# Queries of both mixers projected turned, partitions exchanged by DMA, keys rotated from memory

## The reference

```
h = rms_norm(x); proj = h @ w_in       # 1024 x 3072
a_u, a_v, b_q, b_k, b_v, b_g, c_q, c_k, c_v = split(proj)
y_a = gmlp_mixer(a_u, a_v)             # 4 heads of 64, 128x128 mixing per chunk
y_b = retention_mixer(b_q, b_k, b_v, b_g)   # 6 heads of 64, rope on all 64
y_c = swa_sink_mixer(c_q, c_k, c_v)    # 6 query heads, 2 kv heads, window 128, rope on 16 of 64
x += rms_norm([y_a|y_b|y_c] @ w_out)
x += rms_norm((silu(gate) * up) @ w_ffn_out)
x += sigmoid(x @ w_gate) * rms_norm(p @ w_ple)
```

## Time and profile before

| | |
|---|---|
| median of 3 runs | 1225.25 us |
| profiled execution | 1225.42 us, span 1223.7 us |
| TensorE busy | 1217.0 us, 99% |
| VectorE busy | 841.5 us, 69% |
| ScalarE busy | 616.0 us, 50% |
| GpSimd busy | 136.6 us, 11% |
| HBM read | 118.90 MB, 99 GB/s over the span |

### The profile page before, as it was taken

The page is one execution under the profiler, slowest core; times in us unless marked ns, Lnnn a source line. Parts: engine busy times, 40 slices in busy tenths (PEclk is TensorE's granted clock), DMA queues, the critical chain, the costliest instruction groups (busy, mean ns, idle before and its releaser), DMA issues.

```text
span 1223.7 us, 20397 instructions
## 1 busy us (share of the span) xinstructions
PE 1217.0 (99%) x7873; PEld 1109.8 (91%) x7873; DVE 841.5 (69%) x1365; ACT 616.0 (50%) x1204; POOL 136.6 (11%) x208
## 2 busy tenths in 40 slices
PE   9999999999999999999999999999999999999998
PEld 8988888999999988888899889889999999888887
DVE  5685646888888853267976756468988887433788
ACT  7454435555555532237664544364655555422474
POOL 2003621100000000003030037020000000000120
PEclk9999999999999999999999999999999999999999
DMA  7322232233333354320242222231333333444001
GB/s 247 111 65 91 70 103 69 70 104 104 104 105 106 109 183 154 124 67 18 86 119 73 91 75 90 74 103 53 104 105 106 108 101 119 163 147 172 18 18 70
DMA packets 124464, 122.31 MB, mean 100 GB/s; under 512 B 5200, under 2 KB 108752, under 8 KB 124368
## 3 DMA queue, kind: packets, MB, share of 16 engines
q1 hardware_dynamic: 123680, 120.48, 31.4%
q10 hardware_dynamic: 688, 0.53, 0.2%
HBM read 118.90 MB, written 2.10 MB: 99 GB/s over the span
## 4 chain that ended last, share of the span: by engine, by line
PE 98%; DVE 1%; ACT 0%; POOL 0%; issue 0%; DVEq 0%; ACTq 0%
PE bank L1004 31%; PE bank L1006 30%; PE bank L1005 30%; PE bank L1214 2%; PE bank L1273 1%; PE bank L1294 1%; PE bank L1333 1%; PE bank L1317 1%; PE bank L1309 0%; PE bank L1281 0%; PE bank L1329 0%; PE bank L1338 0%; PE bank L1224 0%; PE bank L1359 0%; PE bank L1255 0%; DVE ple_n L2196 0%
## 5 line engine op out<-in xcount | busy, mean ns | idle before, releaser
L1004 PE MATMUL bank<-w_hi,h_hi 128*128 128x384 f32 (+2 forms) x564 | 200.4, 355 | 0.8 <-DVE w_lo L1893 0.7
L1005 PE MATMUL bank<-w_lo,h_hi 128*128 128x384 f32 (+2 forms) x564 | 194.6, 345 | 0.0
L1891 DVE TENSOR_TENSOR w_lo<-raw,w_hi 128x1024 fp32r<-128x1024 f32 x70 | 83.6, 1233 | 133.7 <-ACT w_hi L1411 133.5
L1004 PE MATMUL bank<-h_hi,w_hi 128*128 128x256 f32 x568 | 161.0, 284 | 0.1
L1006 PE MATMUL bank<-h_hi,w_lo 128*128 128x256 f32 x568 | 160.7, 283 | 0.0
L1005 PE MATMUL bank<-h_lo,w_hi 128*128 128x256 f32 x568 | 160.7, 283 | 0.0
L1006 PE MATMUL bank<-w_hi,h_lo 128*128 128x384 f32 (+2 forms) x468 | 157.5, 336 | 0.0
L1411 ACT ACTIVATE w_hi<-raw 128x1024 fp32r<-128x1024 f32 x70 | 70.6, 1053 | 160.7 <-PE bank L1006 160.6
L1006 PE MATMUL bank<-w_hi,mid_lo 128*128 128x512 f32 x352 | 137.0, 389 | 0.0
L1004 PE MATMUL bank<-T_hi,w_hi 128*128 128x256 f32 x448 | 126.8, 283 | 0.0
L1005 PE MATMUL bank<-T_lo,w_hi 128*128 128x256 f32 x448 | 126.8, 283 | 0.0
(11 more groups left out here) (294 smaller groups left out, 2909.3 us busy)
## 6 DMA issues: line engine op xcount, KB each, us to landing
raw<-in_w_ffn_in SPq DMA_DIRECT2D x88, 512.0 KB, 3.9
raw<-in_w_ffn_out SPq DMA_DIRECT2D x44, 512.0 KB, 4.2
raw<-in_w_in SPq DMA_DIRECT2D x40, 384.0 KB, 3.8
raw<-in_w_out SPq DMA_DIRECT2D x16, 512.0 KB, 3.8
gw<-in_w_gate SPq DMA_DIRECT2D x16, 512.0 KB, 3.4
raw<-in_w_in SPq DMA_DIRECT2D x10, 512.0 KB, 4.6
raw<-in_w_ple SPq DMA_DIRECT2D x4, 512.0 KB, 5.9
x<-in_x_in SPq DMA_DIRECT2D x3, 512.0 KB, 6.9
```

Source lines behind the costliest of these rows:

```text
L1004: pe.matmul(out_ap, a_hi, b_hi, start=start, stop=False, skip_group_check=True)
L1005: pe.matmul(out_ap, a_hi, b_lo, start=False, stop=False, skip_group_check=True)
L1891: last = dve.tensor_tensor(lo, raw[q % RAWS][:, cols], hi, ALU.subtract)
```

## The change

The queries of both mixers are projected turned. On the host the columns of `w_in` are put in another order: a, bk, bv, bg, cq (its heads in pairs), bq, ckv. The 768 query columns make three groups qa, qb, qc of 256, each one strip over all 1024 rows, in place of cq and bq with two strips each; a layer has 12 `w_in` strips where it had 13. In `mm_turned` 128 weight columns are stationary and the tokens, 512 columns of `h_hi` and `h_lo`, move: a block's result has head dimensions on partitions. There are six blocks, in banks 0 to 3 in turn. The order of groups is ckv, qa, qb, qc, bk, bv, a, bg.

ScalarE copies each block to `q_raw`; four transfers by SP write it to `q_turn` with the halves of each head exchanged (8 or 32 partitions each, the rest of `q_turn` is zero from GpSimd); VectorE multiplies q_raw by a table of cosines (ones where nothing rotates), q_turn by a table of signed sines, and adds. The tables, 4 x 256 KB, are new inputs, loaded each layer. Results stand in cT and in the new qT. The norm's scale of the window queries moves from the copy to the exponential's scale and the maximum's factor (`s_q`, `s_qn`, two GpSimd operations for each tile).

`swa_T` transposes only the four tiles of ck, at once, in slot 8; `ret_T` only the keys. bk is copied out by ScalarE and rotated from memory by VectorE (`k_rope`) in slots 24, 26, 30 and 32. The retention's steps stand two slots earlier, gMLP's four and more, and the end of the mixer is rearranged. In the second layer the first block is taken in two parts, columns 0 to 383 (`q_most`) before the last tile of ckv, the rest after it; the conversion of the first query strip is in two halves. The other edits are places in memory and semaphores.

```diff
+    for i in range(2 * len(TURNED)):
+        put((6, 8, 10, 12, 16, 17)[i], "q_rope", i)
+    put(8, "swa_T")
     for c in range(TILES):
-        put(10 + c, "swa_T", c)
...
-            put(u + (1 if c < 3 else 2), "swa_yhi", c - 1)
+            put(u + 1, "swa_yhi", c - 1)
...
-            put(u + (1 if c < 2 else 2), "swa_ylo", c - 1)
+            put(u + (1 if c != 2 else 2), "swa_ylo", c - 1)
         put(u + (2, 1, 2, 2)[c], "swa_norm", c)
+        put(u + (5, 4, 4, 5)[c], "swa_mask", c)
         put(u + 5, "swa_PT", c)
-        put(u + (5, 5, 3, 5)[c], "swa_mask", c)
...
-        u = (33, 37, 41, 45)[c]
+        u = (31, 35, 39, 43)[c]
...
-        put(41 + c, "gmlp_v", c)
-        put(42 + c, "gmlp_n", c)
+        put(37 + c if c < 3 else 41, "gmlp_v", c)
+        put(38 + c if c < 3 else 42, "gmlp_n", c)
+        put((24, 26, 30, 32)[c], "k_rope", c)
     for c in range(TILES):
-        put(48 + c, "ret_norm", c)
-        put(50 + c, "ret_yT", c)
+        put(44 + c if c < TILES - 1 else 48, "ret_norm", c)
+        if c < TILES - 1:
+            put(46 + c, "ret_yT", c)
...
         add("gmlp_mix")
         mm(o[0], 1)
+        add("ret_yT", TILES - 1)
         mm(o[1], 1)
...
             mm(ins[0], 2, nxt)
+            add("q_most", lay=nxt)
+            mm(ins[0], 3, nxt)
             mm(ins[1], 0, nxt)
             mm(ins[1], 1, nxt)
-            mm(ins[0], 3, nxt)
...
+                if 3 <= s < 5:
+                    i = s - 3
+                    if layer:
+                        sp.wait_ge(g_mm, g_count(layer - 1, 4))
+                        sp.wait_ge(x_new, x_count(layer - 1, "gate", 3))
+                    sp.dma_start(cos_q[i][:], turns[2 * i]).then_inc(turns_loaded[i], 16)
+                    sp.dma_start(sin_q[i][:], turns[2 * i + 1]).then_inc(turns_loaded[i], 16)
...
+                if 6 <= s < 6 + len(TURNED):
+                    for i in (2 * s - 12, 2 * s - 11):
+                        b = i % 2
+                        half = HD // 8 if i < 3 else HD // 2
+                        sp.wait_ge(q_evac, 6 * layer + i + 1)
+                        for r in (0, HD):
+                            for d in (r, r + half):
+                                src = 2 * r + half - d
+                                sp.dma_start(q_turn[b][d:d + half, :],
+                                             q_raw[b][src:src + half, :]).then_inc(q_turned[b], 16)
...
+                    if name == "bk":
+                        pe.wait_ge(q_evac, 6 * layer + (5, 6, 3, 4)[m])
...
+            def mm_turned(layer, i, half, cols):
+
+                g = layer * NS + SIDX[("in", TURNED[i // 2], 0)]
+                if half == 0 and i < 4:
+                    pe.wait_ge(*evac(layer, "ckv", i))
+                elif half == 0:
+                    pe.wait_ge(q_evac, 6 * layer + i - 3)
+                pe.wait_ge(h_lo_ready, h_count(layer, "mix", (cols.stop - 1) // P, half))
+                pe.wait_ge(lo_ready, 2 * g + 1 + half)
+                hi, lo = (w[slot_of(g)][:, :].rearrange("p (k c) -> p k c", k=KD) for w in (w_hi, w_lo))
+                c = slice(i % 2 * P, i % 2 * P + P)
+                for k in range(4 * half, 4 * half + 4):
+                    last = mm3(banks[i % 4][:, cols], hi[:, k, c], lo[:, k, c], h_hi[:, k, cols], h_lo[:, k, cols],
+                               k == 0, k == KD - 1)
+                return last
...
+                    if name in TURNED and m % 2:
+                        i = 2 * TURNED.index(name) + m // 2
+                        n = 6 * layer + i + 1
+                        b = i % 2
+                        act.wait_ge(mm_done, mm_count(layer, strip, m))
+                        if n > 2:
+                            act.wait_ge(q_roped, n - 2)
+                        if i < 2:
+                            act.wait_ge(q_zeroed, 2 * layer + i + 1)
+                        act.activation(q_raw[b][:], banks[i % 4][:, :], ACT.Copy).then_inc(q_evac, 1)
...
+                elif kind == "q_rope":
+                    i = e[1]
+                    n = 6 * layer + i + 1
+                    b, which = i % 2, i // 3
+                    dst = (cT, qT)[which][:, i % 3, :]
+                    dve.wait_ge(q_evac, n)
+                    if i % 3 == 0:
+                        dve.wait_ge(turns_loaded[which], 32 * (layer + 1))
+                    dve.tensor_tensor(dst, q_raw[b][:], cos_q[which][:], ALU.mult)
+                    dve.wait_ge(q_turned[b], 64 * (3 * layer + i // 2 + 1))
+                    step(dve.tensor_tensor(q_turn[b][:], q_turn[b][:], sin_q[which][:], ALU.mult))
+                    done(dve.tensor_tensor(dst, dst, q_turn[b][:], ALU.add), q_roped)
```

More of the change, by code:

```diff
@@ L402, in build_trunk @@
                 post_mix, pre_ffn, w_ffn_in, w_ffn_out, post_ffn, w_gate, w_ple, ple_norm,
-                table, later, out):
+                table, later, turns, out):
     KB = 1024
@@ L533, in build_trunk @@
     gmu = small(4)
-    gvar = small(4)
+    gvar = [small(4) for _ in range(2)]
     gvt = small(4)
@@ L577, in build_trunk @@
     evac_act = sem("evac_act")
-    evac_dve = sem("evac_dve")
     ck_roped = sem("ck_roped")
-    cq_roped = sem("cq_roped")
+    turns_loaded = [sem(f"turns_loaded{i}") for i in range(2)]
+    q_evac = sem("q_evac")
+    q_turned = [sem(f"q_turned{i}") for i in range(2)]
+    q_roped = sem("q_roped")
+    q_scaled = sem("q_scaled")
+    q_zeroed = sem("q_zeroed")
     b_roped = sem("b_roped")
@@ L1161, in block_of @@
                     pe.wait_ge(lo_ready, 2 * (g + 1))
-                if kind == "in":
+                if kind == "in" and strip[1] in TURNED:
+                    block = 2 * TURNED.index(strip[1]) + m // 2
+                    last = mm_turned(layer, block, m % 2, slice(S - P if layer and block == 0 else 0, S))
+                elif kind == "in":
                     last = mm_in(layer, g, strip, m)
@@ L1246, in _ @@
                     gate_product(layer, e[1], e[2:] or (0, 1))
+                elif kind == "q_most":
+                    for half in range(2):
+                        mm_turned(layer, 0, half, slice(0, S - P))
                 elif kind == "swa_T":
[L1249 to L1258, removed]
+                    pe.wait_ge(ck_roped, (layer + 1) * TILES)
+                    for c in range(TILES):
+                        last = pe.transpose(banks[6][:, c * P:(c + 1) * P], ck[:, c, :], T_("ident"))
+                    last.then_inc(swa_T, 1)
                 elif kind in ("swa_cur", "swa_prev"):
@@ L1306, in _ @@
                         pe.wait_ge(y_lo_ready, y_count(layer, ("swa_o", 2)))
[L1307 to L1310, removed]
+                    for j in range(3):
+                        last = pe.transpose(banks[4][:, j * P:(j + 1) * P], bk[:, c, j * P:(j + 1) * P], T_("ident"))
                     last.then_inc(ret_T, 1)
@@ L2385 @@
     depth = w_in.shape[0]
-    table, later = small_tables()
+    table, later, turns = small_tables()
     values = {
@@ L2396 @@
         "w_gate": w_ple_gate, "w_ple": w_ple_proj, "ple_norm": ple_norm,
[L2397 removed]
+        "table": table, "later": later, "turns": turns,
     }
```

163 lines of the change are left out of this document (89 added, 74 removed).

## The result

The changed kernel takes 1231.44 us, the median of 9 runs (1227.22 to 1233.47), the kernel before 1225.25 (9 runs, 1225.08 to 1225.55). The ratio is 1.0043, 95% interval 1.0033 to 1.0052: slower. I had forecast 1220.9, range 1219.2 to 1224.0, and given "slower" 0.08. The profiled execution took 1231.63 us with a span of 1229.5.

What follows compares the result with a forecast made beforehand. TensorE, busy 1217.0 of 1223.7 us, was taken to bound the kernel. Its savings of 3.13 and 1.84 us by layer (-4.97), plus 0.6 for holes, gave -4.4: a median of 1220.9 us, range 1219.2 to 1224.0.

Steps and rivals of the forecast that it cites:

- The sum without the hole ahead of ret_yT: TensorE's savings on query products and transposes less the split block's cost: -3.13 us first layer, -1.84 second, -4.97 together.
- my +0.6: End of the mixer: TensorE waits 0.3 us a layer for y_lo of tile 0 before tile 1's ret_yT, +0.6 in all.
- The 14 ns fixed part: TensorE: each product pays 0.014 us whatever its columns; 48 fewer query products a layer save 0.67 us.
- rival (d): Query products on TensorE: fixed part not saved with 512-column moving queries, -0.24 in place of -1.34, 1222.0 us; chance 0.05.
- (c): Second layer's split block: short products cost as much as whole ones, +4.2 instead of +1.29, 1223.8 us; chance 0.06.
- (e): No holes anywhere, and the split block's short products at 0.0725 us each: -5.8 us, 1219.5 us; chance 0.14.
- rival (a): q_turn transfers land late, so TensorE waits at slot 17; at 9.3 us landing time +5.0, 1230.2 us; chance 0.11.
- (b): Small holes: slot 17 or the last transposes expose about 1 us a layer more, 1222.9 us; chance 0.14.
- L: Landing time of a query block's transfers inside SBUF, taken as 3 us; no hole until 4.6.
- The cover at slot 17: bk's product with tile 1 needs block 5's bank, copied out behind tile 0's exponentials; 1.1 us to spare.
- The step that failed: VectorE and ScalarE lose 8 query rotations, gain 18 operations; keys rotated in slots 24 to 32 for use from 31.
- the split's 1.29 us: Second layer's first block in two parts costs TensorE +1.29 us, with 24 short products at 0.107 each.

Runs made afterwards that it cites:

- the keys in the gaps: The changed kernel with the four key rotations moved to the ends of slots 24, 24, 29 and 29, where VectorE stood idle: 1221.0 us, ratio 0.9963.
- The run: The changed kernel with key rotations in VectorE's idle time, and the second layer's first query block taken whole, no filler ahead: 1219.77 us, ratio 0.9954.
- the nine added ones: The kernel before with nine unused 384-column VectorE operations ahead of the first retention tile's masking in each layer: 1239.51 us, ratio 1.0114.

## Why the prediction was wrong

**The terms on TensorE were right.** The sum without the hole ahead of ret_yT was -3.13 us for the first layer and -4.97 for both. With the keys in the gaps the second layer's first transpose starts at 608.23, in the kernel before at 611.31: -3.08. The span goes from 1223.7 to 1218.9: -4.8. The execution gains 4.5, since the part outside the span grew from 1.7 to 2.1. The 1221.0 of that version is the forecast's time, 1220.9, partly by luck: my +0.6 for a hole ahead of the ret_yT of tile 1 was not there (in that version they start at 159.54 without idle time; y_lo of tile 0 ends 2.1 after ret_o 3, from 157.10 to 159.23, where I had 2.8, since ret_norm 2 stands behind it and not ahead of it), and the 0.4 outside the span was not in my sum. The 14 ns fixed part, rival (d), stands; the short products, rivals (c) and (e), cost 24 x 0.110.

**The transfers were covered**, rival (a) and the first half of (b). TensorE waits for nothing at slot 17. Block 2's copy ends at 40.44 in the changed kernel, SP issues its four transfers from 40.47 to 43.12, and they have landed at 44.47, when VectorE starts its sine product: L was 1.35 us where I took 3 (a block of 16 KB pieces; for those of 64 KB VectorE waits for nothing), and an issue 0.66 from start to start where I took 0.43. (The 2.0 us that the prediction quotes from the Trainium skill, DMA: Bandwidth & Descriptors, "Anatomy of one DMA", is given there for transfers that GpSimd issues; SP issued these.) The cover at slot 17 was thinner than my 1.1 us. In both layers block 5's copy ends 0.47 us ahead of it, because the six exponentials ahead of the copy take 0.48 us each and not 0.39:

```profile
44.47 0.69 DVE L2319 TENSOR_TENSOR q_turn<-q_turn,sin_q 128x512 f32<-128x512 f32 x1 [1.37 <-DMA q_turn<-q_raw]
...
58.11 0.58 ACT L1789 ACTIVATE q_raw<-bank 128x512 f32<-128x512 f32 x1
...
59.16 0.33 PE L1044 MATMUL bank<-w_hi,h_hi 128*128 128x384 f32 x1
```

**The step that failed** is the sentence "VectorE and ScalarE lose 8 query rotations of cq and bq and gain 18 operations of 512 columns; keys are rotated from memory in slots 24 to 32 for use from 31". It says by when the keys are needed, and puts what their rotation does to VectorE's queue at nothing. I counted VectorE's work as a sum and worked out its queue at slots 13 to 17 and at the end of the mixer only. At slot 33 two moves meet. The window attention keeps its slots and the retention's come two earlier, so ret_o 0 follows more closely on the softmax of tile 3, the same queue's work: from that tile's mask on VectorE to the moment when TensorE asks for scm it was 19.5 us (92.16 to 111.67) and is 15.2 (98.83 to 114.07). And two rotations, 1.6 us (113.68 to 115.27) and, slowed, 2.8 (105.91 to 108.7), come in between. The row of the kernel before at 107.61 held the slack: scm ended 3.0 us ahead of ret_o 0. It was not among my rows. With the slack at 3.0 us and 4.3 of the distance gone, TensorE's wait for scm was to be asked for. The earlier start alone opens no hole, though: with the rotations in the gaps scm ends at 112.27, 1.25 us ahead of ret_o 0. It is the two moves together that do, and easing either closes it: the rotations moved into the gaps, or the output one slot later.

**The second failure is the price.** Every rival had a hole at its own length: (a) as "L - 4.6 a layer", the range's upper end the same. The hole that came, 2.27 us, cost 5.7 in the first layer. With the right hole and my price the time would have been 1221.0 + 5.0 = 1226.0, where 1231.4 was measured. The range of 1224.0 at the top could hold neither.

The Trainium skill, TensorE: Matmul & The Clock Gate, "HAM oscillation — how this bites in real kernels", warns that gaps of TensorE cost clock besides themselves. The rows here agree in kind (0.50 granted from about 116.9 to 123.7), though the gaps of the section's example are longer than these. I should have carried it as a rival to every hole.

**The filler.** I wrote that TensorE asks for tile 3's low part "only after the 24 filler products" and took the split's 1.29 us as the price of hiding something. The run shows it hid nothing. The row was there: VectorE's low part ended at 625.59, ahead of 626.33, where the filler began; the filler had nothing to cover in the kernel before either.

## What to carry to other kernels

When a change moves the consumer earlier and puts work into the producer's queue, write down that queue at the moved step, in order, with each wait; a sum of work over the stage says nothing. Put work that has slack into the producer's idle time in front of the tight step (here 2.78 us behind y_lo), never between the tight step and the wait that releases it. And where the bound engine is TensorE, price a hole of about 2 us at more than its length (1.7 to 2.5 times here), and as unsteady from run to run.

## What the runs showed of the hardware

- The granted clock was 0.50 behind holes of 1.71, 2.25, 2.27 and 4.02 us, in the executions that were traced, and 1.00 behind those of 0.3; with holes of 1.71 and 2.27 the mean clock of the whole run was 1.000 in two runs of ten and two of nine.
- An exponential of 128 columns takes 0.48 us with its scale from a column of memory and 0.39 with a number. The Trainium skill, ScalarE: Activation LUTs, "What ACT_TABLE_LOAD costs", gives about 93 ns for each such operand; the runs agree, and six of them in a row before a tight step are half a microsecond of the hole.
- VectorE's operations that read two operands from memory slow down beside GpSimd: 0.36 to 0.87 and 0.98 us (106.96 and 107.75, beside GpSimd's products from 106.63 to 108.52), a conversion of four from 2.20 to 3.34, the nine added ones 0.79 each in place of 0.55. The Trainium skill, GPSIMD Engine Reference, "1. Specifications", names the shared interface for operations with two inputs from memory; the trace agrees, and scm, which reads one operand from a bank, kept its time: 1.01 in the kernel before, beside GpSimd's products of 107.23 and 108.14, and 1.02 in the changed kernel with GpSimd idle.
